# A mixture-of-experts stage with twelve weight slots instead of six, and the first two experts loaded ahead

## The chip, the core and the metric

The kernel runs on one core of one Trainium2 chip. A core has five engines that run their own instruction streams and meet at semaphores: PE (matrix products; its weight loads are listed apart as PEld), DVE (vector), ACT (activations and copies), POOL and SP, which here issues nearly all transfers from device memory. Sixteen DMA engines carry the transfers. The metric is the time of one execution in microseconds (us) on the device, a median of several.

## What is computed

One inference step of a two-layer backbone over 384 tokens (128 context, 256 latent) with a model width of 1024. Each layer is a mixer (attention and a convolution branch, merged by gates) and then a mixture of experts. All data are f32. The part that matters here is the second one:

```python
def moe(h, w_router, router_bias, w_gate, w_up, w_down):
    t = h.reshape(B * L, D)                                  # 384 x 1024
    scores = jax.nn.sigmoid((t @ w_router).astype(jnp.float32))
    ...                                                      # 1 of 4 groups, top 2 of its 4 experts
    combine = jnp.einsum('tk,tke->te', w, jax.nn.one_hot(eidx, N_EXPERTS, dtype=jnp.float32))
    hid = jax.nn.silu(jnp.einsum('td,edf->tef', t, w_gate)) * jnp.einsum('td,edf->tef', t, w_up)
    hid = hid * combine.astype(hid.dtype)[..., None]
    return jnp.einsum('tef,efd->td', hid, w_down).reshape(B, L, D)
```

There are 16 experts (0 to 15) a layer, each with a gate, an up (1024 x 512) and a down (512 x 1024) matrix: 6 MB an expert, 96 MB a layer, 192 MB in all of the 302 MB that the kernel reads.

## The kernel before

**Stages of a layer.** One hardware loop runs over the two layers, so the code of a layer stands once in every engine's program and is run twice. The stages are: adaLN (`ada`), the input projection (`qkv`, `u`, `gate`), attention with the gate products between its steps, the convolution branch, `aproj` and `cproj`, `out`, then routing (a norm, router logits, a rank of every token within its experts, and `spread`, which sorts the tokens by expert into `sortedT`), then the experts.

**Weights.** All weights pass through `ring`, six tiles of 1 MB (128 partitions x 2048 f32). The mixer's weights are cut into 48 chunks (`CHUNKS`), chunk c goes to slot c mod 6. An expert is six chunks j: gate in slots 0 and 1, up in 2 and 3, down in 4 and 5. SP issues the loads in the program's order; before each it waits until the slot's previous chunk has been used (`half` counts the uses that end in the middle of a product, `full[b]` the products that end in PSUM bank b). So chunk j of expert e waits for chunk j of expert e - 1. Expert 0 loads as the last mixer chunks are used up, in `out` and routing (L468 to L470). `landed[s]` tells PE that a slot is filled.

**An expert on PE** (`expert`, L889). Its tokens were copied by ACT to `xgT`. `products(0, 2)` multiplies them by the gate matrix, `products(1, 3)` by the up matrix, `turn_own` and `turn_hid` transpose small tiles, `down` multiplies by the down matrix. Between these, `sums` (`back`, L597) adds the rows of the expert before to the tokens' sums, so that PE doesn't wait for ACT and DVE. An expert with at most 64 tokens is *narrow* (two half-width products side by side, L557), else *wide* (L560). Since an expert's code depends on its own width and on that of the expert before, `by_width` (L370) reads two flags and branches, and the program of a pass holds four variants, in this order: narrow after narrow, narrow after wide, wide after narrow, wide after wide. Expert 0 stands in front of the loop in two variants, the loop (L919) runs experts 1 to 15, one in a pass. At its end stands the branch back.

**DVE and ACT** have loops of their own over the experts, with two variants each.

**What lies where.** `over` lays a second name on a tile that is dead by then: `hid`, `silu`, `hidT` and `own` of the expert stage lie in the convolution's tiles `csq` and `conv`, `xgT` in `probs`. The mixer's other tiles (`sig`, `hT`, `qkv`) hold nothing late in the expert stage, or only part of it.

Of the kernel before, what the change touches and what calls it, by code (L numbers as in the profile page):

```python
# [24 lines left out]
P = 128  # L25
D = 1024
# [40 lines left out]
assert NCHUNKS % SLOTS == 0  # L67
SLOT_USES = (NCHUNKS + MOE_CHUNKS * NE) // SLOTS

# [30 lines left out]

START = 3

# [28 lines left out]
def build(nc, A):  # L131
    USES, INIT, MOE_AT, PER = bank_table()
    ctx = ExitStack()
    with ctx:
        start_of = {}

        def sb(name, shape, dt=F32):
            start_of[name] = (nc.sbuf_base + 31) // 32 * 32
            return ctx.enter_context(nc.sbuf_tensor(name, shape, dt))
# [19 lines left out]
        conv = sb("conv", [P, KC, CO])  # L159
        csq = sb("csq", [P, KC, CO])  # L160
        mix = sb("mix", [P, 2 * KD * T + 4 * T])
        gates = mix[:, 0:2 * KD * T].rearrange("p (m n) -> p m n", n=T)
# [109 lines left out]

        landed = [sem(f"landed{s}") for s in range(SLOTS)]
        full = [sem(f"full{b}") for b in range(8)]
        freed = [sem(f"freed{b}") for b in range(8)]
# [141 lines left out]
        def _(sp):  # L417
# [7 lines left out]

            def load(slot, landed_sem, src):
                n = src.shape[-1]
                k = src.shape[-2]
                dst = ring[slot][:, 0:k * n].rearrange("p (k n) -> p k n", k=k)
                sp.dma_start(dst, src).then_inc(landed_sem, 16)  # L430
# [12 lines left out]
            with sp.Fori(0, DEPTH) as l:  # L443
                for c in range(NCHUNKS):
                    s = c % SLOTS
                    if c < SLOTS:

                        if c in (0, 2, 4):
                            sp.wait_ge(half, l * HALF_PER + {0: START - 2, 2: START - 1, 4: START}[c])
                        else:  # L450
                            b = {1: 2, 3: 3, 5: 6}[c]
                            sp.wait_ge(full[b], l * PER[b] + INIT[b] - (2 if c in (1, 3) else 0))
                    else:
                        wait_chunk_used(c - SLOTS, l)
                    kind, i, part = CHUNKS[c]
                    if kind == "ada":
                        src = w_ada[bass.ds(l, 1), part, :, :, i * 512:(i + 1) * 512].rearrange("o p k n -> p (o k) n")
                    elif kind in ("aproj", "cproj"):
                        w = w_ap if kind == "aproj" else w_cp
                        src = w[bass.ds(l, 1), :, :, i * 512:(i + 1) * 512].rearrange("o p k n -> p (o k) n")  # L460
                    elif kind == "router":
                        src = w_r
                    else:
                        w = w_out if kind == "out" else w_in
                        m = i + {"qkv": 0, "u": 3, "gate": 7, "out": 0}[kind]
                        src = w[bass.ds(l, 1), :, :, m * 256:(m + 1) * 256].rearrange("o p k n -> p (o k) n")
                    load(s, landed[s], src)
                for j in range(MOE_CHUNKS):  # L468
                    wait_chunk_used(NCHUNKS - SLOTS + j, l)
                    load(j, landed[j], expert_chunk(j, l * NE))  # L470

                def reload(e, first=False):
                    for j in range(MOE_CHUNKS):
                        if j in (0, 2, 4):
                            sp.wait_ge(half, l * HALF_PER + e * 3 + (12 + START - 3 + {0: 1, 2: 2, 4: 3}[j]))
                        elif j in (1, 3):
                            b = {1: 2, 3: 3}[j]
                            sp.wait_ge(full[b], lead(b, l, e - 1, first) + 1)
                        else:
                            sp.wait_ge(full[6], l * PER[6] + e + (INIT[6] + MOE_AT[6]))  # L480
                        load(j, landed[j], expert_chunk(j, l * NE + e))

                reload(1, True)
                with sp.Fori(2, NE) as e:
                    reload(e)

# [4 lines left out]
                with sp.If(over > 0):  # L491
# [3 lines left out]
                    with sp.Fori(0, BLOCKS - 1) as q:  # L495
                        with sp.Fori(0, NE) as e:
                            for j in range(MOE_CHUNKS):
# [7 lines left out]
                                load(j, landed_o[j], expert_chunk(j, l * NE + e))  # L505

# [17 lines left out]
        def _(pe):  # L524
# [20 lines left out]

            def expert_parts(n_of, lead_of, fr, fs, landed_s, land_at, half_s, own_s, own_at, xg_s, xg_at):

                def products(which, b, small):
                    pe.wait_ge(fr[b], lead_of(b))
                    pe.wait_ge(xg_s, xg_at)  # L550
                    for k in range(KD):
# [3 lines left out]
                        if small:  # L555
                            for hh in range(2):
                                last = pe.matmul(ps[64 * hh:64 * hh + 64, b, 0:256], xgT[:, k, 0:64],  # L557
                                                 ring[s][:, o + hh * 256:o + (hh + 1) * 256], start=(k == 0), stop=(k == KD - 1))
                        else:
                            last = pe.matmul(ps[:, b, :], xgT[:, k, :], ring[s][:, o:o + DE], start=(k == 0), stop=(k == KD - 1))  # L560
                        if k % 4 == 3:
# [16 lines left out]
                def down(small):  # L578
# [3 lines left out]
                    for k in range(KE):  # L582
# [3 lines left out]
                        for h in range(2):  # L586
                            w = ring[4 + s][:, c * D + h * 512:c * D + (h + 1) * 512]
                            a, z, rows = (64 * h, 64 * h + 64, hidT[:, c, 64 * s:64 * s + 64]) if small else (0, P, hidT[:, k, :])
# [34 lines left out]
            with pe.Fori(0, DEPTH) as l:  # L623
# [264 lines left out]
                settle(pe)  # L888
                def expert(e, before_e=None):  # L889
                    alone = before_e is None  # L890
                    products, turn_own, turn_hid, down = expert_parts(
                        lambda b: expert_use(b, l, e), lambda b: lead(b, l, e, alone), freed, full, landed,
                        l * (16 * SLOT_USES) + (e * 16 + 16 * 9), half, own_r, l * NE + (e + 2), xg_r, l * (NE + 1) + (e + 2))

# [30 lines left out]
                with pe.If(over > 0):  # L925
# [5 lines left out]
                    with pe.Fori(0, OSTEPS) as i:  # L931
                        products, turn_own, turn_hid, down = expert_parts(
                            lambda b: further_use(b, l, i), lambda b: further_use(b, l, i), freed_o, full_o, landed_o,
                            l * (16 * OSTEPS) + i * 16 + 16, half_o, own_r_o, l * OSTEPS + i + 2, xg_r_o, l * OSTEPS + i + 1)
# [906 lines left out]
```

## Time and profile before

| | us |
|---|---|
| three runs: median (lowest to highest) | 1324.78 (1319.63 to 1330.17) |
| the profiled execution: time | 1327.07 |
| its span (first to last instruction) | 1325.4 |
| PE busy in the span | 1187.1 |
| DVE busy | 702.0 |
| ACT busy | 433.7 |

The profile is of one execution. Stages can be told by line: L680 and L694 are the mixer's products, L878 is `spread`, L557 and L560 an expert's gate and up products, L589 its down product, L612 the sums. In the first layer the expert stage runs from 379 to 650 us, in the second from 1018 to 1293. "Chain" below is the chain of work that ended last, followed back from the end: a row is a start, a duration, and the engine and line, or the transfer, that held it. "Issue" is time in which an engine waited for nothing that the profile shows. In a timeline row the brackets hold the engine's idle time before it and what ended it. The granted clock of TensorE (PEclk) is given as a share of full speed.

### The profile page before, as it was taken

The page shows a single profiled execution, that of the slowest core. Times are in us where ns is not written, and L with a number is a line of the kernel's source. Part 1 is how long each engine was busy: PE and PEld are TensorE (multiplying, and loading weights), DVE is VectorE, ACT ScalarE, POOL GpSimd, SP SyncE. Part 2 cuts the span into 40 slices and gives each one's busy share as a digit, 9 for nine tenths or more (in the row PEclk, how much of TensorE's full clock was granted, in tenths as well). Part 3 has the DMA queues.
Part 4 walks back from the last instruction along what each step waited for, and adds up shares of the span by engine and source line. Part 5 has one row for each costly group of instructions (what it writes and reads, how often), then busy time and mean ns, then how long its engine had stood idle before and what let it go on. Part 6 is the DMA issues. An engine that isn't in the chain of part 4 may idle for free.

```text
span 1325.4 us, 20656 instructions
## 1 busy us (share of the span) xinstructions
PE 1187.1 (90%) x6340; PEld 755.7 (57%) x6341; DVE 702.0 (53%) x1425; ACT 433.7 (33%) x771; POOL 9.8 (1%) x30
## 2 busy tenths in 40 slices
PE   5999999998579999999689999999958899999973
PEld 2796555588354455444369755557926454455443
DVE  4365877664722344444566387767464234244445
ACT  2425555442331122222152345544233222122213
POOL 1000000000000000000000000000000000000000
PEclk8899999999699999999799999999978999999996
DMA  8743655423146899999783265552320889889961
GB/s 312 227 130 123 227 190 177 142 66 127 38 158 228 317 387 422 422 421 422 273 285 108 87 221 182 174 187 66 127 69 27 307 348 423 322 320 423 422 260 48
DMA packets 101983, 305.36 MB, mean 230 GB/s; under 512 B 7136, under 2 KB 47824, under 8 KB 77328
## 3 DMA queue, kind: packets, MB, share of 16 engines
q1 hardware_dynamic: 99248, 301.62, 61.0%
q10 hardware_dynamic: 2528, 2.50, 0.6%
q8 instruction: 40, 0.66, 0.2%
q14 instruction: 39, 0.32, 0.1%
q0 software_dynamic: 128, 0.26, 0.1%
HBM read 302.53 MB, written 1.84 MB: 230 GB/s over the span
## 4 chain that ended last, share of the span: by engine, by line
PE 69%; DMA 15%; DVE 8%; issue 4%; ACT 4%; DVEq 0%; SPq 0%; ACTq 0%
PE ps L694 14%; DMA ring<-in_w_e_up 13%; PE ps L557 9%; PE ps L589 6%; PE ps L560 6%; PE ps L680 5%; PE ps L715 4%; PE ps L716 3%; PE ps L717 3%; PE ps L612 3%; PE ps L878 3%; PE ps L641 2%; PE ps L653 2%; PE ps L785 2%; PE ps L760 1%
## 5 line engine op out<-in xcount | busy, mean ns | idle before, releaser
L557 PE MATMUL ps<-ring,xgT 128*64 128x256 f32 x1728 | 205.7, 387 | 16.5 <-issue 10.6
L557 PEld LDWEIGHTS ps<-ring,xgT 128*64 128x64 f32 x1728 | 125.9, 138 | 103.1 <-issue 27.7
L1420 DVE SCALAR_TENSOR_TENSOR nat<-ps,qT,nat 128x512 f32<-128x512 f32 x192 | 132.8, 745 | 80.6 <-PE ps L612 80.6
L694 PE MATMUL ps<-hT,ring 128*128 128x384 f32 x512 | 173.4, 492 | 0.0
L589 PE MATMUL ps<-ring,conv 128*64 128x512 f32 (+1 forms) x512 | 134.2, 597 | 7.2 <-issue 4.1
L1527 DVE SCALAR_TENSOR_TENSOR conv<-ub,dw,conv 128x414 f32<-128x414 f32 x240 | 136.6, 644 | 0.0
L694 PEld LDWEIGHTS ps<-hT,ring 128*128 128x128 f32 x512 | 95.4, 191 | 66.4 <-issue 7.2
L1411 DVE TENSOR_TENSOR orow_lo<-ps,orow_hi 64x512 fp32r<-64x512 f32 (+1 forms) x64 | 44.1, 689 | 112.5 <-ACT orow_hi L1037 111.7
L589 PEld LDWEIGHTS ps<-ring,conv 128*64 128x64 f32 (+1 forms) x512 | 48.3, 145 | 78.5 <-issue 78.2
L1402 DVE TENSOR_TENSOR csq<-csq,ps 128x256 f32<-128x256 f32 (+1 forms) x32 | 14.8, 463 | 129.4 <-PE ps L557 83.8
L560 PE MATMUL ps<-ring,xgT 128*128 128x512 f32 x160 | 74.8, 624 | 8.4 <-issue 8.4
L1027 ACT ACTIVATE conv<-ps 128x256 f32<-128x256 f32 (+1 forms) x32 | 13.4, 419 | 194.6 <-PE ps L575 194.6
L680 PE MATMUL ps<-ring,hT 128*128 128x256 f32 x288 | 65.9, 393 | 3.1 <-DVE hT L1377 3.1
L1037 ACT ACTIVATE orow_hi<-ps 64x512 fp32r<-64x512 f32 (+1 forms) x64 | 37.9, 593 | 87.7 <-PE ps L589 87.0
L680 PEld LDWEIGHTS ps<-ring,hT 128*128 128x128 f32 x288 | 56.8, 198 | 11.6 <-DVE hT L1377 3.4
L612 PE MATMUL ps<-orow_hi,ownT 64*128 64x512 f32 (+1 forms) x192 | 53.1, 501 | 7.6 <-DVE orow_lo L1411 4.5
L560 PEld LDWEIGHTS ps<-ring,xgT 128*128 128x128 f32 x160 | 31.2, 199 | 49.4 <-issue 48.0
L641 PE MATMUL ps<-ring,condT 128*32 128x512 f32 x384 | 51.0, 651 | 5.0 <-DMA ring<-in_w_ada 5.0
L1024 ACT ACTIVATE csq<-ps 128x256 f32<-128x256 f32 (+1 forms) x32 | 13.4, 418 | 123.8 <-PE ps L557 83.5
L715 PE MATMUL ps<-merged_hi,w_hi 128*128 128x384 f32 x128 | 43.7, 341 | 5.1 <-DVE merged_lo L1605 5.1
L878 PE MATMUL ps<-place,nat_hi 128*128 128x384 f32 x96 | 35.5, 370 | 13.7 <-DVE place L1708 13.7
L1111 ACT ACTIVATE mix<-ps 128x384 f32<-128x384 f32 x32 | 15.7, 492 | 90.2 <-PE ps L694 90.2
(254 smaller groups left out, 1797.3 us busy)
## 6 DMA issues: line engine op xcount, KB each, us to landing
ring<-in_w_e_gate SPq DMA_DIRECT2D x64, 1024.0 KB, 10.1
ring<-in_w_e_up SPq DMA_DIRECT2D x64, 1024.0 KB, 10.8
ring<-in_w_e_down SPq DMA_DIRECT2D x64, 1024.0 KB, 9.8
ring<-in_w_ada SPq DMA_DIRECT2D x48, 1024.0 KB, 7.7
ring<-in_w_in SPq DMA_DIRECT2D x30, 1024.0 KB, 6.1
ring<-in_w_out SPq DMA_DIRECT2D x8, 1024.0 KB, 5.9
ring<-in_w_attn_proj SPq DMA_DIRECT2D x4, 1024.0 KB, 5.6
ring<-in_w_conv_proj SPq DMA_DIRECT2D x4, 1024.0 KB, 6.6
```

The source lines that it names most:

```text
L557: last = pe.matmul(ps[64 * hh:64 * hh + 64, b, 0:256], xgT[:, k, 0:64], ring[s][:, o + hh * 256:o + (hh + 1) * 256], start=(k == 0), stop= ...
L560: last = pe.matmul(ps[:, b, :], xgT[:, k, :], ring[s][:, o:o + DE], start=(k == 0), stop=(k == KD - 1))
L589: last = pe.matmul(ps[a:z, 5 + h, :], rows, w, start=(k == 0), stop=(k == KE - 1))
L612: last = pe.matmul(ps[:, b, :], ownT[a:z, t * P:(t + 1) * P], rows[a:z, o:o + 512], start=first, stop=not first)
L641: last = pe.matmul(ps[32 * k:32 * k + 32, b, :], condT[:, 4 * cc + k, :], ring[c % SLOTS][:, k * 512:(k + 1) * 512], start=(cc == 0), stop ...
L680: last = pe.matmul(ps[:, b, 0:256], hT[:, k, t * P:(t + 1) * P], ring[q % SLOTS][:, k * 256:(k + 1) * 256], start=(k == 0), stop=(k == KD ...
L694: last = pe.matmul(ps[:, b, 0:T], ring[c % SLOTS][:, o:o + P], rhs(k), start=(k == 0), stop=(k == k_tiles - 1))
L715: pe.matmul(ps[:, b, 0:T], upper, hi[:, k, 0:T], start=(k == 0), stop=False)
L878: last = pe.matmul(ps[:, b, 0:HALF], part[:, t, k * P:(k + 1) * P], place[:, t, half_at * HALF:(half_at + 1) * HALF], start=(i == 0), stop ...
L1411: dve.tensor_tensor(orow_lo[a:z, o:o + 512], ps[a:z, 5 + h, :], orow_hi[a:z, o:o + 512].bitcast(F32), ALU.subtract).then_inc(fr[5 + h], 1)
L1420: dve.scalar_tensor_tensor(sums, ps[:, b, :], weight[:, t, bass.ds(at, 1)], sums, ALU.mult, ALU.add).then_inc(fr[b], 1)
L1527: dve.scalar_tensor_tensor(conv[:, i, :], src, w, conv[:, i, :], ALU.mult, ALU.add).then_inc(tapped, 1)
```

## The change

A second set of six 1 MB tiles, `odd`, is laid over tiles that are dead in the expert stage (`sig` with the start of the convolution's tiles, `probs` with what follows, `hT`, the end of `qkv`). Even experts use `ring`, odd experts `odd`, with their own semaphores `landed_odd`. Chunk j of expert e now waits for chunk j of expert e - 2. The first odd expert's chunks load as soon as what lies there is dead: after attention's last product, after `cproj`, after the second norm, after `spread`. `hid`, `silu`, `hidT`, `own` and `xgT` move to other dead places. The loops of PE and SP run over pairs of experts and hold two bodies; on PE, expert 1 stands in front of the loop as well. `START`, from which some semaphores begin to count, goes from 3 to 8, with the constants that follow from it.

```diff
-SLOT_USES = (NCHUNKS + MOE_CHUNKS * NE) // SLOTS
+SLOT_USES = NCHUNKS // SLOTS + NE // 2
...
-START = 3
+START = 8
...
-        hid = flat(csq, 0, DE)
-        silu = flat(csq, DE, 2 * DE)
-        hidT = flat(conv, 0, DE).rearrange("p (k n) -> p k n", k=KE)
-        own = flat(conv, DE, DE + NT * P).rearrange("p (t n) -> p t n", t=NT)
+        hid = over("hid", "qkv", 0, [P, DE], F32)
+        silu = over("silu", "qkv", DE, [P, DE], F32)
+        hidT = over("hidT", "qkv", 3 * D + NT * P, [P, KE, P], F32)
+        own = over("own", "hT", NT * ROWS, [P, NT, P], F32)
...
-        xgT = over("xgT", "probs", 0, [P, KD, P], F32)
+        xgT = over("xgT", "qT", 2 * NT * BLOCKS * NE, [P, KD, P], F32)
...
+        odd = [over("odd0", "sig", 0, [P, SLOT], F32), over("odd1", "sig", SLOT, [P, SLOT], F32),
+               over("odd2", "probs", 0, [P, SLOT], F32), over("odd3", "probs", SLOT, [P, SLOT], F32),
+               over("odd4", "hT", 0, [P, SLOT], F32), over("odd5", "qkv", 3 * D + NT * P + DE, [P, SLOT], F32)]
...
-                for j in range(MOE_CHUNKS):
-                    wait_chunk_used(NCHUNKS - SLOTS + j, l)
-                    load(j, landed[j], expert_chunk(j, l * NE))
-
-                def reload(e, first=False):
+                def first_even(j):
+                    wait_chunk_used(NCHUNKS - SLOTS + j, l)
+                    load(ring[j], landed[j], expert_chunk(j, l * NE))
+
+                def first_odd(j):
+                    if j == 2:
+                        b, n = use("pv", UNITS - 1, l)
+                        sp.wait_ge(full[b], n + 1)
+                    elif j < 2:
+                        b, n = use("cproj", KD - 1, l)
+                        sp.wait_ge(full[b], n + 1)
+                    elif j == 3:
+                        sp.wait_ge(xn_r, l * (2 * KD) + 2 * KD)
+                    else:
+                        b, n = use("spread", 2 * KD - 1, l)
+                        sp.wait_ge(full[b], n + 1)
+                    load(odd[j], landed_odd[j], expert_chunk(j, l * NE + 1))
+
+                first_odd(2)
+                first_even(0)
+                first_odd(0)
+                first_odd(1)
+                for j in range(1, 5):
+                    first_even(j)
+                first_odd(3)
+                first_even(5)
+                first_odd(4)
+                first_odd(5)
+
+                def reload(e, before_e, tiles, landed_s, first=False):
...
-                reload(1, True)
-                with sp.Fori(2, NE) as e:
-                    reload(e)
+                reload(2, 0, ring, landed, True)
+                reload(3, 1, odd, landed_odd)
+                with sp.Fori(2, NE // 2) as i:
+                    reload(i * 2, i * 2 - 2, ring, landed)
+                    reload(i * 2 + 1, i * 2 - 1, odd, landed_odd)
...
-                def expert(e, before_e=None):
+                def expert(e, pair, odd_one, before_e=None):
                     alone = before_e is None
+                    if odd_one:
+                        tiles, landed_s, land_at = odd, landed_odd, l * (16 * NE // 2) + (pair * 16 + 16)
+                    else:
+                        tiles, landed_s, land_at = ring, landed, l * (16 * SLOT_USES) + (pair * 16 + 16 * (NCHUNKS // SLOTS + 1))
...
-                expert(0)
-                with pe.Fori(0, NE - 1) as e:
-                    expert(e + 1, e)
+                expert(0, 0, False)
+                expert(1, 0, True, 0)
+                with pe.Fori(1, NE // 2) as i:
+                    expert(i * 2, i, False, i * 2 - 1)
+                    expert(i * 2 + 1, i, True, i * 2)
```

PE's program at the end of a loop pass, before the change: the last rows of the wide-after-wide variant (its down product), the branches out of it, and the branch back to the loop's start.

```order
L612 MATMUL ps<-orow_lo,ownT 128x512 x2
L579 REGISTER_ALU
L581 ISA x2
L589 MATMUL ps<-ring,conv 128x512 x8
L375 UNCONDITIONAL_BRANCH x2
L919 REGISTER_ALU
L919 COMPARE_AND_BRANCH
```

And of the change, the same place in the even body: behind the same down product stands not the loop's end but the odd body, with its two flag reads and branches and its first variant on the odd tiles.

```order
L628 MATMUL ps<-ring,hidT 128x512 x8
L385 UNCONDITIONAL_BRANCH x2
L382 ISA
L382 TENSOR_LOAD narrow_e
L382 ISA x2
L383 COMPARE_AND_BRANCH
L382 TENSOR_LOAD narrow_e
L382 ISA x2
L383 COMPARE_AND_BRANCH
```

The loop's end with its branch back has moved one whole body of four variants further from the loop's start, and every even expert now ends with a jump to this middle. Each of the two bodies holds four variants of the kind of which the rows below show the narrow-after-narrow one (odd tiles).

```order
L596 MATMUL ps<-odd_77,xgT 64x256 x8
L596 MATMUL ps<-odd_78,xgT 64x256 x8
L651 MATMUL ps<-orow_hi,ownT 128x512 x2
L651 MATMUL ps<-orow_lo,ownT 128x512 x2
...
L607 MATMUL ps<-ident,own 128x128 x3
...
L614 MATMUL ps<-ident,hid 128x128 x2
...
L628 MATMUL ps<-odd_81,hidT 64x512 x4
L628 MATMUL ps<-odd_82,hidT 64x512 x4
```

Its rows are those of before, with other tiles: nothing is added inside a variant, the variants are doubled.

SP's program between the router's weights and the first reload, before:

```order
L430 DMA ring<-in_w_router 128x8x16
...
L430 DMA ring<-in_w_e_gate 128x2048
...
L430 DMA ring<-in_w_e_up 128x2048
...
L430 DMA ring<-in_w_e_down 128x2048
```

and of the change (77 to 82 are the odd tiles 0 to 5):

```order
L440 DMA ring<-in_w_router 128x8x16
L486 REGISTER_ALU
L440 ISA
L440 DMA odd_79<-in_w_e_up 128x2048
L434 REGISTER_ALU
L440 ISA
L440 DMA ring<-in_w_e_gate 128x2048
L440 DMA odd_77<-in_w_e_gate 128x2048
L440 ISA
L440 DMA odd_78<-in_w_e_gate 128x2048
```

Before, six loads stood here, all of expert 0; now twelve stand here in turns, six of expert 0 and six of expert 1, and SP waits at each until its place is dead.

## Rows read from the trace of the kernel before

**Rows 1.** Page part 4: shares of the chain by engine and by line.

```profile
PE 69%; DMA 15%; DVE 8%; issue 4%; ACT 4%; DVEq 0%; SPq 0%; ACTq 0%
```

**Rows 2.** Chain in order of time, first layer's expert stage: start us, us, what.

```profile
393.39 5.97 issue
399.36 9.35 PE ps L560 x16
...
440.77 7.06 PE ps L560 x16
...
479.90 3.45 PE ps L557 x32
...
515.19 12.87 DMA ring<-in_w_e_up
...
619.55 13.00 DMA ring<-in_w_e_up
...
636.76 3.63 PE ps L589 x15
```

**Rows 3.** Chain in order of time, second layer's expert stage.

```profile
1018.04 15.71 PE ps L560 x32
...
1057.76 5.26 issue
1063.02 5.14 PE ps L557 x32
...
1088.23 3.65 PE ps L589 x16
...
1101.82 3.65 PE ps L589 x16
...
1183.32 3.45 PE ps L557 x32
...
1280.52 3.63 PE ps L589 x15
```

**Rows 4.** Busy time by stretch, columns in the first row.

```profile
core 0: us, PE busy (x) PEld busy (x) DVE busy (x) ACT busy (x) POOL busy (x), PEclk, DMA share, GB/s
20.00:370.00 350.00, 319.72 (x1582) 230.37 (x1583) 228.70 (x477) 146.01 (x264) 3.11 (x5) 0.94 0.45 151
...
399.30:426.20 26.90, 26.44 (x69) 11.38 (x69) 5.06 (x8) 3.24 (x5) 0.00 (x0) 0.92 0.58 199
...
501.00:632.60 131.60, 123.78 (x860) 63.77 (x858) 59.52 (x108) 30.57 (x54) 0.00 (x0) 1.00 1.01 422
...
281.00:377.00 96.00, 74.54 (x393) 65.56 (x391) 57.10 (x145) 31.55 (x50) 1.86 (x3) 0.88 0.21 69
```

**Rows 5.** DMA queues, whole span, then 20 to 370 us: packets, MB, share.

```profile
q8 instruction: 40, 0.66, 0.2%
...
q8 instruction: 13, 0.21, 0.2%
```

**Rows 6.** DMA queues, 393 to 399.5 us.

```profile
q8 instruction: 2, 0.03, 2.7%
```

**Rows 7.** DMA queues, 399.5 to 440 us.

```profile
q8 instruction: 2, 0.03, 0.3%
```

**Rows 8.** DMA queues, 440 to 650 us, all rows.

```profile
q1 hardware_dynamic: 13456, 83.47, 98.3%
q14 instruction: 3, 0.02, 0.0%
```

**Rows 9.** DMA queues, 1057 to 1063 us.

```profile
q8 instruction: 1, 0.02, 0.9%
```

**Rows 10.** Timeline of SP's queue, 280 to 400 us: two loads of each kind.

```profile
289.54 11.47 SPq L430 DMA_DIRECT2D ring<-in_w_e_gate  x2
...
382.39 2.68 SPq L430 DMA_DIRECT2D ring<-in_w_e_gate  x2
```

**Rows 11.** Timeline of PE, where the layer loop turns back.

```profile
657.88 0.71 PE L628 MATMUL ps<-ident,prow 76*128 76x76 f32 x2 [3.18 <-DVE xT L1791]
```

More of the change, by code:

```diff
@@ L160, in build @@
         csq = sb("csq", [P, KC, CO])
+        gap = sb("gap", [P, 16])
         mix = sb("mix", [P, 2 * KD * T + 4 * T])
@@ L273, in build @@
         landed = [sem(f"landed{s}") for s in range(SLOTS)]
+        landed_odd = [sem(f"landed_odd{s}") for s in range(SLOTS)]
         full = [sem(f"full{b}") for b in range(8)]
@@ L424, in wait_chunk_used, with load @@
                     sp.wait_ge(full[b], n + 1)
-            def load(slot, landed_sem, src):
+            def load(tile, landed_sem, src):
                 n = src.shape[-1]
                 k = src.shape[-2]
-                dst = ring[slot][:, 0:k * n].rearrange("p (k n) -> p k n", k=k)
+                dst = tile[:, 0:k * n].rearrange("p (k n) -> p k n", k=k)
                 sp.dma_start(dst, src).then_inc(landed_sem, 16)
@@ L466, in _ @@
                         src = w[bass.ds(l, 1), :, :, m * 256:(m + 1) * 256].rearrange("o p k n -> p (o k) n")
-                    load(s, landed[s], src)
-                for j in range(MOE_CHUNKS):
+                    load(ring[s], landed[s], src)
+                def first_even(j):
                     wait_chunk_used(NCHUNKS - SLOTS + j, l)
-                    load(j, landed[j], expert_chunk(j, l * NE))
-                def reload(e, first=False):
+                    load(ring[j], landed[j], expert_chunk(j, l * NE))
@@ L476, in reload @@
                         elif j in (1, 3):
                             b = {1: 2, 3: 3}[j]
-                            sp.wait_ge(full[b], lead(b, l, e - 1, first) + 1)
+                            sp.wait_ge(full[b], lead(b, l, before_e, first) + 1)
                         else:
-                            sp.wait_ge(full[6], l * PER[6] + e + (INIT[6] + MOE_AT[6]))
-                        load(j, landed[j], expert_chunk(j, l * NE + e))
-                reload(1, True)
-                with sp.Fori(2, NE) as e:
-                    reload(e)
+                            sp.wait_ge(full[6], l * PER[6] + before_e + (INIT[6] + MOE_AT[6] + 1))
@@ L488, in _ @@
+                        load(tiles[j], landed_s[j], expert_chunk(j, l * NE + e))
+                reload(2, 0, ring, landed, True)
[3 more added lines that the diff above has]
+                    reload(i * 2 + 1, i * 2 - 1, odd, landed_odd)
                 sp.wait_ge(pos_r, l + 1)
@@ L504, in _ @@
                                     sp.wait_ge(full_o[b], l * (OSTEPS * back_to) + q * (NE * back_to) + e * back_to + 1)
-                                load(j, landed_o[j], expert_chunk(j, l * NE + e))
+                                load(ring[j], landed_o[j], expert_chunk(j, l * NE + e))
                     sp.wait_ge(full_o[6], l * OSTEPS + (OSTEPS + 1))
@@ L557, in products @@
                                 last = pe.matmul(ps[64 * hh:64 * hh + 64, b, 0:256], xgT[:, k, 0:64],
-                                                 ring[s][:, o + hh * 256:o + (hh + 1) * 256], start=(k == 0), stop=(k == KD - 1))
+                                                 tiles[s][:, o + hh * 256:o + (hh + 1) * 256], start=(k == 0), stop=(k == KD - 1))
                         else:
-                            last = pe.matmul(ps[:, b, :], xgT[:, k, :], ring[s][:, o:o + DE], start=(k == 0), stop=(k == KD - 1))
+                            last = pe.matmul(ps[:, b, :], xgT[:, k, :], tiles[s][:, o:o + DE], start=(k == 0), stop=(k == KD - 1))
                         if k % 4 == 3:
@@ L586, in down @@
                         for h in range(2):
-                            w = ring[4 + s][:, c * D + h * 512:c * D + (h + 1) * 512]
+                            w = tiles[4 + s][:, c * D + h * 512:c * D + (h + 1) * 512]
                             a, z, rows = (64 * h, 64 * h + 64, hidT[:, c, 64 * s:64 * s + 64]) if small else (0, P, hidT[:, k, :])
```

17 lines of the change are left out of this document (10 added, 7 removed).

## The prediction

> **What bounds the kernel now.** I read the chain of waits first: PE holds 69% of the span and transfers 15%, and nearly all of the transfers are one line, `ring<-in_w_e_up`, a weight load of the expert loop [rows 1]. So only the expert stage waits for weights, and I read that stage in order of time.
>
> In the first layer experts 1 and 3 are wide (L560), the rest narrow. From 515.19 to 619.55 the chain shows eight waits for an up-projection chunk, one per expert, seven steps of (619.55 - 515.19) / 7 = 14.9 us [rows 2]. In that stretch the DMA engines are full: 422 GB/s, share 1.01 [rows 4]. So 14.9 us is what six 1 MB chunks take, and the stage is transfer-bound there. Before it, it is not: from one narrow expert's down-projection to the next, 1088.23 to 1101.82, are 13.59 us with only PE rows in the chain [rows 3]. That is the whole room: **a narrow expert costs 14.9 us behind transfers and 13.59 us behind PE.**
>
> Two holes in the same stage are neither: 5.97 us at 393.39 between experts 0 and 1 of the first layer, 5.26 us at 1057.76 between experts 1 and 2 of the second, both marked "issue" [rows 2, 3]. They are not late weights: expert 1's gate chunks were issued from 382.39 [rows 10], and 11 us at this rate are over four chunks. What does fall into both holes is a packet or two on q8, the queue that brings instructions [rows 6, 9]. I take them for PE waiting for its program; the rest of the forecast hangs on that.
>
> **How PE gets its program, as the trace shows it.** 20 to 370 us has no loop: 1582 matmuls and 1583 weight loads ran and 13 packets of 16 KB came [rows 4, 5]. That is 243 records a packet, about 256 with waits and register instructions; I call that a block. A plain f32 matmul row of the program leaves two matmuls and two weight loads in the trace, the others one of each. So a narrow variant of an expert (40 plain rows, 17 others) is 194 records, about 217 instructions, a wide one (24 and 19) about 157. A pass of the loop of before has four variants: about 767 instructions, 3.0 blocks.
>
> First passes: in the first layer PE leaves expert 0's narrow code and leaps over some 570 instructions to "wide after narrow": hole of 5.97 and two packets [rows 2, 6]. In the second it leaves "narrow after wide" and leaps over both wide variants, some 320 instructions, to the loop's end: hole of 5.26 and one packet [rows 3, 9]. A leap over one variant left no hole: expert 1's wide code to the loop's end, 157. So what is fetched ahead is about one block; a leap past it waits. After the first passes nothing is fetched again: two packets more up to 440 [rows 7], none from 440 to 650 [rows 8], ten and more passes. A pass of three blocks stays in PE's store.
>
> **The change, part by part.**
>
> *Twelve slots: takes the transfer-bound stretches away.* Chunk j of expert e+2 can now load as soon as expert e has used its slot, so transfers may run a whole expert ahead. Fourteen experts after the start are 14 x 14.9 = 209 us, the stage is over 260; behind wide experts, which take some 25 us, the transfers gain 10 us on PE and then lose 1.3 us per narrow one, at most 12 x 1.3 = 16 us, less than the expert they may be ahead. So PE sets the pace throughout. First layer: 479.90 to 636.76 + 3.63 = 640.39 is 160.5 us for experts 5 to 15; at 13.59 it is 149.5: **-11.0**. Second layer: 1183.32 to 1280.52 + 3.63 = 1284.15 is 100.8 for seven; at 13.59 it is 95.1: **-5.7** [rows 2, 3]. Together -16.7.
>
> *First two experts loaded early: 0.* The six extra loads fall into 281 to 377 us, where the queue moves 69 of 422 GB/s [rows 4]; expert 0's were there already, from 289.54 [rows 10], and expert 1 waits for no weights now, as shown above. SP's new waits (attention's last product, cproj's last, the norm, the last spread) hold back only loads that wait for something later anyway: behind the last of them stand expert 2's, which need expert 0's products. If that cover were gone, a chunk is 14.9 / 6 = 2.5 us.
>
> *Tiles laid elsewhere, next layer's first w_ada loads one expert earlier: 0.* DVE's and ACT's programs keep their instructions and waits.
>
> *Two bodies in PE's loop, and expert 1 written out in front of it: new first-pass holes.* A pass is now about 1530 instructions, 6.0 blocks, and has a middle as well as an end to leap to. First layer:
> - expert 0 to 1: some 565 instructions, as before: 0.
> - 1 to 2: over one variant: 0.
> - 2 to 3: "narrow after wide" (even) leaps over both wide variants to the middle, some 320, as at 1057.76: 5.3. Then, in the odd body, over both narrow variants (434) to "wide after narrow": the block after the first, and the one after that. One hole of 5.97 if they come together, two of 5.3 if one after the other; I take 8.
> [...]
>
> Second layer (experts 0 wide, 1 to 5 narrow): 1 to 2 leaps over both wide ones, as before: 0 more. Expert 2 is "narrow after narrow", the first variant of the even body, and leaps over the other three (531) to the middle: 5.97; expert 3 the same in the odd body to the loop's end: 5.97. Clock: a narrow first product takes 5.14 instead of 3.45 [rows 3], 1.7 twice. Sum 15.3. First layer 5.3 + 8 + 2.3 = 15.6. Together **+30.9**.
>
> Sum: 1325.4 - 16.7 + 30.9 = **1339.6, say 1340 us**. The median of the three runs, 1324.78, is within a microsecond of this span.
>
> *Bounds of the holes.* Below: nothing, since two of the fetches up to 440 cost nothing, PE's queue running ahead of them; then 1308.7. The nearest cheaper row is the 3.18 us of PE at 657.88, where the layer loop turns back [rows 11]: five blocks at that price plus 5.7 for the clock are 21.6, 1330. Above: every leapt block by itself at 5.3, and expert 1's entry one block worse: three blocks, 2.3 and 5.3 in the first layer, four blocks and 3.4 in the second: 48, 1357. The value taken is that of the rows with like leaps under like traffic.
>
> **Rivals.**
> - *No new holes* (faster). PE's queue runs ahead far enough, or the holes were something that the change doesn't multiply: 1325.4 - 16.7 = 1308.7. For it: the leap of 157 behind a wide expert. Against it: narrow experts, from which the new leaps start, left two of two in the open. It decides for "faster" if the new holes sum to less than 3.5 us.
> - *Cheap holes*: 1330, by the row at 657.88. For it: there the queues were not full of weights. Against: in the expert stage they are.
> - *The pass doesn't stay in PE's store* (much slower). A pass of 6.0 blocks touches seven, and one more is fetched ahead; the trace shows five held, no more. If the first are gone at the loop's turn, each pass has two holes of 5.97, one of 5.3 and three slow products: 22.3 us, twelve more passes in two layers: 268, some 1600. Against it: nothing was fetched twice so far.
>
> [...]
>
> **How the numbers follow.** Likeliest 0.55 (1332 to 1357 by itself), no new holes 0.16, cheap ones 0.14, refetching 0.15. The range 1309 to 1357 leaves out refetching and a tail of the first rival. One per cent, about what can be told here from no change, is 1312 to 1338. Faster: most of the no-hole case, 0.11. Same: the rest of it, the cheap case and two fifths of the likeliest, 0.41. Slower: three fifths of the likeliest and refetching, 0.48. The likeliest case ends just above the bound.
>
> **What would show it.** In the profile after: no `in_w_e_up` waits in the chain; narrow experts 13.6 us apart to the end of both layers; "issue" holes of 5 to 6 us between experts 2 and 3 in both layers and behind 3 in the second, with q8 packets in them; some 52 q8 packets in all (40 now plus six blocks a layer), against some 130 if passes are refetched. The forecast is wrong if the holes are missing, if transfers still wait in the chain, or if q8 keeps running past expert 4.

## The result and the profile after

| | before | changed |
|---|---|---|
| median (lowest to highest) of four runs each on one chip, us | 1325.71 (1319.63 to 1330.17) | 1341.45 (1334.31 to 1345.60) |
| the profiled execution: time, us | 1327.07 | 1334.31 |
| its span, us | 1325.4 | 1332.7 |

The ratio is 1.0129, 95% interval 1.0100 to 1.0158: the changed kernel is slower by about 1.3%, where 1340 us was forecast. The profiled execution of the changed kernel is the quickest of its four, so its rows account for 7.3 us of a difference of 15.7 us in the medians. A second profile, among the experiments, shows where more of it lies.

First the page of the changed kernel: its share of the chain by engine, which answers to [rows 1], and its instruction queue, which answers to [rows 5] (packets, MB, share).

```profile
PE 82%; DVE 7%; issue 5%; ACT 3%; DMA 2%; DVEq 0%; SPq 0%; ACTq 0%
...
q8 instruction: 52, 0.85, 0.3%
```

The transfers fell from 15% of the chain to 2%, and no up-projection load is left in it. "Issue" rose by a point, and twelve more packets of program came. Next the chain of the changed kernel in order of time (start us, us, what), first layer's expert stage, which answers to [rows 2]. Its L596, L599 and L628 are L557, L560 and L589 of before.

```profile
380.23 8.81 PE ps L596 x64
...
394.43 5.33 issue
399.76 9.36 PE ps L599 x16
...
440.87 11.47 issue
452.34 8.67 PE ps L599 x16
...
611.69 3.65 PE ps L628 x16
...
625.28 3.65 PE ps L628 x16
...
638.86 3.63 PE ps L628 x15
```

The old hole between experts 0 and 1 is there (5.33), and a new one between experts 2 and 3, 11.47 us long. Later the narrow experts follow each other at 625.28 - 611.69 = 13.59 us, the pace of PE, in place of the 14.9 us behind transfers. The second layer, which answers to [rows 3]:

```profile
1018.38 15.71 PE ps L599 x32
...
1058.09 3.40 issue
1061.49 3.67 PE ps L596 x32
...
1075.30 5.75 issue
1081.05 6.56 PE ps L596 x32
...
1097.74 5.59 issue
1103.33 5.67 PE ps L596 x32
...
1287.78 3.63 PE ps L628 x15
```

Two new holes, behind experts 2 and 3, and behind each a first product of 5.7 to 6.6 us where 3.45 is normal. The instruction queue of the changed kernel from 440.9 to 452.3 us, the hole of the first layer:

```profile
q8 instruction: 4, 0.07, 2.7%
```

From 473.25 to 649.5 us, nearly all the rest of the first layer's stage, the same view has no q8 row, only these:

```profile
q1 hardware_dynamic: 11985, 71.10, 99.0%
q14 instruction: 2, 0.02, 0.0%
```

So the code is fetched once a layer and then stays: in the second layer no q8 row stands from 1110 to 1290 us either. The busy time of the stretch that [rows 4] show of before (us, PE busy, PEld, DVE, ACT, POOL, granted clock, DMA share, GB/s):

```profile
501.00:632.60 131.60, 129.70 (x936) 73.92 (x935) 64.65 (x118) 33.67 (x60) 0.00 (x0) 1.00 1.01 422
```

PE is busy 129.7 of 131.6 us, where it was 123.8. The transfers run as full as before, but now they run ahead of PE and nothing waits for them.

**Where the time went.** I measure the expert stage from the start of expert 0's first product (the L596 x64 and L599 x32 rows) to the end of the last down product (the x15 rows), in the chain of each profile:

| profile | first layer, us | second layer, us | sum | span |
|---|---|---|---|---|
| before | 261.2 | 266.1 | 527.3 | 1325.4 |
| changed | 262.3 | 273.0 | 535.3 | 1332.7 |
| changed, second profile | 262.3 | 276.3 | 538.6 | 1336.5 |
| changed, late loads | 262.1 | 279.8 | 542.0 | 1342.9 |
| before, two bodies | 273.2 | 278.8 | 552.0 | 1349.7 |
| before, short branches | 253.4 | 259.2 | 512.6 | 1311.6 |
| changed, short branches | 242.7 | 253.7 | 496.4 | 1291.5 |

The span less both stages is 798.1 us before and 797.4 after: whatever the change moved outside the expert stages costs nothing that can be seen.

### The profile page after: what moved, and what is told of

The parts are those of the page before. It is cut to its first block, busy times and chain, and to the rows that moved or that the text cites. A ratio compares the mean times of both kernels' runs of the same rounds, so it can differ in the third digit from the quotient of the medians.

```text
span 1332.7 us, 20562 instructions
## 1 busy us (share of the span) xinstructions
PE 1184.2 (89%) x6340; PEld 761.8 (57%) x6341; DVE 702.3 (53%) x1425; ACT 434.0 (33%) x771; POOL 9.7 (1%) x30
## 4 chain that ended last, share of the span: by engine, by line
PE 82%; DVE 7%; issue 5%; ACT 3%; DMA 2%; DVEq 0%; SPq 0%; ACTq 0%
PE ps L596 15%; PE ps L733 14%; PE ps L628 10%; PE ps L599 6%; PE ps L651 5%; PE ps L719 5%; PE ps L754 4%; PE ps L755 3%; PE ps L756 3%; PE ps L917 3%; PE ps L680 3%; PE ps L692 2%; PE ps L824 2%; PE ps L799 1%; PE ps L869 1%
## 5 line engine op out<-in xcount | busy, mean ns | idle before, releaser
L596 PE MATMUL ps<-ring,xgT 128*64 128x256 f32 x896 | 106.2, 391 | 11.0 <-issue 11.0
L596 PE MATMUL ps<-odd,xgT 128*64 128x256 f32 x832 | 98.1, 389 | 5.8 <-issue 5.8
L596 PEld LDWEIGHTS ps<-ring,xgT 128*64 128x64 f32 x896 | 68.2, 141 | 51.3 <-issue 26.5
L596 PEld LDWEIGHTS ps<-odd,xgT 128*64 128x64 f32 x832 | 64.0, 140 | 42.0 <-issue 20.3
L1447 DVE TENSOR_TENSOR hid<-silu,ps 128x256 f32<-128x256 f32 (+1 forms) x32 | 14.8, 463 | 119.6 <-PE ps L596 73.9
L1072 ACT ACTIVATE hidT<-ps 128x256 f32<-128x256 f32 (+1 forms) x32 | 13.4, 418 | 185.2 <-PE ps L614 185.2
L628 PE MATMUL ps<-odd,hidT 128*64 128x512 f32 (+1 forms) x256 | 68.8, 597 | 2.9 <-issue 2.2
L628 PE MATMUL ps<-ring,hidT 128*64 128x512 f32 (+1 forms) x256 | 65.4, 597 | 4.0 <-ACT hidT L1072 2.1
L599 PE MATMUL ps<-odd,xgT 128*128 128x512 f32 x96 | 46.4, 639 | 16.8 <-issue 16.8
L628 PEld LDWEIGHTS ps<-odd,hidT 128*64 128x64 f32 (+1 forms) x256 | 25.1, 146 | 39.6 <-issue 38.7
```

The source lines that it names most:

```text
L599: last = pe.matmul(ps[:, b, :], xgT[:, k, :], tiles[s][:, o:o + DE], start=(k == 0), stop=(k == KD - 1))
L628: last = pe.matmul(ps[a:z, 5 + h, :], rows, w, start=(k == 0), stop=(k == KE - 1))
```

## Experiments

**Theory.** The change is two changes. The twelve slots are worth some 17 us; the way PE's program was written for them, two long bodies a pass, costs some 25 to 31 us in first passes, because branches leap over code that has not been fetched yet. **Rival:** the holes belong to the weights (odd tiles, earlier loads, late chunks). The expectations count the experts from the first, which is expert 0.

### The code without the slots: two bodies in the kernel before

```diff
-                with pe.Fori(0, NE - 1) as e:
-                    expert(e + 1, e)
+                expert(1, 0)
+                with pe.Fori(1, NE // 2) as i:
+                    expert(i * 2, i * 2 - 1)
+                    expert(i * 2 + 1, i * 2)
```

> The kernel before with six slots and its old loads; only the code of TensorE's expert loop is changed: two experts' bodies in one pass of the loop, and the second expert in front of it. No weight comes earlier or later by design. Theory (holes are code that is not yet on the chip): the long branch leaps of a first pass come back in a new place, as in the changed kernel: in the first layer one hole of 8 to 13 us before the fourth expert, in the second layer two of 5 to 6 us, each with 1.5 to 3 us of low clock behind it; since the rest of the stage is bound by the transfers, part of it is soaked up: 1335 to 1352 us, ratio 1.008 to 1.02, some 50 instruction packets on TensorE's queue. Rival (the holes belong to the new buffers and late weights): no new hole, 1325 us, ratio 0.998 to 1.002.

Measured: 1350.89 us against 1323.87 for the kernel before on the same chip, ratio 1.0205 (1.0167 to 1.0244), 52 instruction packets. Its chain, first and second layer:

```profile
438.57 11.50 issue
450.08 8.76 PE ps L560 x16
...
525.81 12.71 DMA ring<-in_w_e_up
...
1088.80 4.48 issue
...
1109.65 5.44 issue
```

With six slots and the old loads the holes appear between the same experts and at nearly the same lengths as in the changed kernel (11.50 for 11.47; 4.48 and 5.44 for 5.75 and 5.59). So the holes come with PE's code, not with the new tiles. The stages grew by 12.0 and 12.7 us, where the new holes, the slow products behind them and what changed in the old ones sum to 12.9 and 13.5. So the transfers that bind the rest of the stage (12.71 at 525.81) soaked up less than a microsecond in each, and the part of the expectation on soaking up was wrong. A transfer waits for a slot that PE frees late, which may be why; no run singles that out.

### The same work in short branches

Each step of an expert gets a two-way branch of its own, in place of one choice among four whole variants: seven two-way branches an expert in place of two. A pass shrinks by half (in the changed kernel from some 1530 to some 790 instructions), and no branch leaps far. Made twice, on the changed kernel and on the kernel before:

```diff
-                    if alone:
-                        by_width(pe, e, lambda small: whole(small, None))
-                    else:
-                        by_width(pe, e, lambda small: by_width(pe, before_e, lambda small_before: whole(small, small_before)))
+                    narrow = pe.value_load(narrow_e[0:1, bass.ds(e, 1)], min_val=0, max_val=1)
+                    if not alone:
+                        narrow_before = pe.value_load(narrow_e[0:1, bass.ds(before_e, 1)], min_val=0, max_val=1)
+                    def either(flag, step):
+                        with pe.If(flag > 0):
+                            step(True)
+                        with pe.Else():
+                            step(False)
+                        pe.nop()
...
+                    either(narrow, lambda small: products(0, 2, small))
+                    add_before(0)
+                    either(narrow, lambda small: products(1, 3, small))
+                    add_before(1)
+                    turn_own()
+                    either(narrow, turn_hid)
+                    add_before(2)
+                    either(narrow, down)
```

> The changed kernel; only TensorE's code is changed: instead of four whole variants of each expert (wide or narrow after wide or narrow), each step of an expert has its own two-way branch, so that a pass has some 790 instructions instead of 1530 and no branch jumps over more than some 70. Theory (long jumps over code not yet fetched): all idle time of kind issue between the experts 1 to 4 goes, in both layers, with its low clock (11.5 + 1.6 + 5.3 in the first, 5.8 + 5.6 + 3.4 + 5.3 in the second, 38 us of the quickest run): 1296 to 1306 us. If the added branches themselves cost 0.1 to 0.3 us each and lie bare (about 7 more per expert, 32 experts): 1320 to 1365. Rival (the holes are late weights or rows): they stay, about 1341.

> The kernel before with the same short branches on TensorE and nothing else. Theory: the old holes of the first experts go (6.0 in the first layer, 5.3 in the second, with 3 to 4 us of low clock), and the steady experts stay at the pace of the transfers, which also hides the added branches: 1308 to 1318 us, ratio 0.987 to 0.994. Rival (those holes are something else): 1325, ratio 0.998 to 1.002.

Measured on the same chip: 1294.23 us for the changed kernel with short branches, 2 us below the expected range, ratio to before 0.9779 (0.9744 to 0.9813); 1313.23 for the kernel before with them, ratio 0.9907 (0.9870 to 0.9944). The chain of the changed kernel with short branches, where the holes were:

```profile
389.15 3.65 PE ps L628 x16
392.81 7.07 PE ps L599 x16
...
428.53 3.58 PE ps L628 x16
432.11 7.06 PE ps L599 x16
...
481.38 3.65 PE ps L628 x16
...
495.00 3.65 PE ps L628 x16
```

Expert 1's first product follows expert 0's last at once and takes 7.07, not 9.36; expert 3 follows expert 2 at once. The steady step, 495.00 - 481.38 = 13.62 us for 13.59, shows that the five branches more an expert cost next to nothing. In the kernel before with short branches the same places are closed, and the transfers are the bound from 511 us on, their waits ending at 523.91 and 538.83, at the old step of 14.9 us:

```profile
511.42 12.49 DMA ring<-in_w_e_up
...
525.94 12.89 DMA ring<-in_w_e_up
```

These four kernels split the result. Slots: 1294.23 - 1313.23 = -19.0 us in the medians, -10.7 and -5.6 in the stages. Code: +24.7 us in the stages of the two-body kernel. Their sum, -16.3 + 24.7 = +8.4, is what the changed kernel's profile shows, +8.0. And the version with both, slots and short branches, beats the kernel before by 2.2%.

### Early loads of the second expert taken back

```diff
-                first_odd(2)
-                first_even(0)
-                first_odd(0)
...
+                for j in range(6):
...
+                b, n = use("spread", 2 * KD - 1, l)
+                sp.wait_ge(full[b], n + 1)
+                for j in range(6):
+                    first_odd(j)
```

> The changed kernel with the second expert's six loads all issued after the spread, behind the first expert's six, instead of between them. Theory (loading the second expert early is worth nothing, since it waits for the code and then lags behind by one expert): as the changed kernel within 3 us, 1338 to 1345 us. Rival (the early load carries part of the time): the second expert waits for its weights about 10 us in each layer, 1350 to 1361 us, with idle time that ends by a DMA in the chain before the second expert.

Measured: 1343.43 us, ratio 1.0133 (1.0087 to 1.0179), where the changed kernel has 1.0129. SP's timeline of this kernel shows all six loads between 378.30 and 381.6:

```profile
378.30 0.86 SPq L440 DMA_DIRECT2D odd<-in_w_e_gate  x2
...
380.48 1.09 SPq L440 DMA_DIRECT2D odd<-in_w_e_down  x2
```

The first layer's stage is 262.1 us against 262.3. A wait of expert 1 for its weights could still be hidden by the hole in front of it, so the same edit was made where that hole is gone, on top of the short branches:

> Both edits together: short branches on TensorE, and the second expert's six loads issued only after the spread, behind the first expert's. Without the hole in front of it the second expert starts 7 us earlier than in the changed kernel, so its weights could now be the last thing to come. If early loading is worth nothing even then (six loads issued at 378 land two or three us apart, the gate chunks before the first expert is done at 393): as with early loads, 1292 to 1299 us, no transfer in the chain between the first two experts. If it carries something: a wait that a transfer ends in front of the second expert, 3 to 12 us a layer, 1300 to 1318 us. If it is worth less than nothing (the early loads take transfer time from the mixer's last weights): 1280 to 1291 us.

Measured: 1295.67 us, ratio 0.9789 (0.9753 to 0.9825), against 1294.23 and 0.9779 with early loads, and no transfer in the chain between the first two experts. Loading the second expert early is worth nothing here in either form: the other six slots are free after the spread, and six loads issued then are in time.

### The variants in another order

The even body's variants in reverse order of code, wide after wide first:

```diff
...
+                            with pe.If(narrow < 1):
+                                step(False)
+                            with pe.Else():
+                                step(True)
...
-                    expert(i * 2, i, False, i * 2 - 1)
+                    expert(i * 2, i, False, i * 2 - 1, turned=True)
```

> The changed kernel with the four variants of the even experts' body in the opposite order of code (wide after wide first, narrow after narrow last); the work is the same. Theory (a hole stands where a branch leaps over code that is not there yet): in the second layer the third expert's variant now ends where the fourth expert's code begins, so the hole of 5.75 us between them goes, and one of 8 to 12 us opens between the second and the third, where there were 3.4 us, since three variants are leapt over there; the one behind the fourth expert stays (5 to 6, or 12 us). In the first layer a hole of 4 to 8 us opens between the second and third expert, where there was none, and that between the third and fourth shrinks from 11.5 to 4 to 8 us. Time 1333 to 1350 us. Rival (the place in the order of experts decides, by weights or rows): holes stay between the same experts at the same lengths.

Measured, one execution: 1336.18 us (the changed kernel on that chip 1338.11). The chain of this kernel:

```profile
443.22 5.60 issue
...
1053.01 11.01 issue
...
1076.39 3.65 PE ps L628 x16
1080.05 3.45 PE ps L596 x32
...
1093.63 10.97 issue
```

The holes moved with the code, at the same experts, weights and rows. In the second layer expert 3 (1080.05) follows expert 2 at once, where 5.75 us stood; in front of expert 2 the hole grew from 3.40 to 11.01. In the first layer the one behind expert 2 shrank from 11.47 to 5.60. One part missed: in front of the first layer's expert 2 a hole of 4 to 8 us was expected, and none came, though three wide variants are leapt there (expert 1's own last one and two of the body). Expert 1 is wide in that layer and takes some 26 us. A packet of program moved at 423.91, 4.8 us before it was done, so the fetch may have been hidden behind its work; no run tests that.

### A pass longer by a fifth, never run

```diff
...
+                            for _ in range(75):
+                                pe.matmul(ps[:, 2, :], xgT[:, 0, :], tiles[0][:, 0:DE], start=True, stop=True)
...
```

It stands in the even body's wide-after-wide variant, which this data never takes.

> The changed kernel with 75 more matmuls (300 instructions) in one variant of the loop's even body that this data never takes, so that nothing more is computed: a pass grows from 1530 to 1831 instructions of code. If the store of TensorE's code still holds the whole pass: as the changed kernel, 1335 to 1352 us, 53 to 58 instruction packets on TensorE's queue, none late in a loop. If the pass no longer fits: packets in every pass, 100 to 170 in all, holes in the chain in each of the seven passes, 1450 to 1600 us. [...]

Measured, one execution: 1557.41 us, 219 us above the changed kernel on that chip, and 149 packets instead of 52. Its chain in the first layer, long after the first pass, and its instruction queue from 520 to 671 us:

```profile
520.15 6.48 issue
526.62 5.53 PE ps L596 x32
...
542.28 12.71 issue
...
593.15 12.52 issue
...
643.99 11.84 issue
```

```profile
q8 instruction: 27, 0.44, 1.5%
```

From the middle of the first layer's third pass on (520.15), and in the passes of the second layer, the code is fetched again, and PE waits at the middle and at the end of a pass. One pass of narrow experts, from 593.15 to 643.99, is 50.84 us, where two steps of 13.59 are 27.18: with the slow products a refetched pass costs 23.7 us more. (The 219 us are 18 a pass over the twelve passes behind the first ones of the two layers.) One part missed: holes were expected in each of the seven passes, but the first layer's second pass (experts 4 and 5) ran without a hole, and no packet moved from 473 to 520 us. Why that pass was spared stays open. Otherwise a pass of some 1530 instructions stays (no packet from 473.25 to 649.5 us in the changed kernel), and one of some 1830 doesn't (27 packets from 520 to 671 us here). The longer leap in the even body is not all of it: behind the odd body (12.52 at 593.15), whose own leaps are as long as before, PE waits as well, though the jump back from there is longer too.

### The holes without weight traffic

The loads of the experts 2 to 15 cut to 64 of 2048 columns:

```diff
-                        load(tiles[j], landed_s[j], expert_chunk(j, l * NE + e))
+                        sp.dma_start(tiles[j][:, 0:64], expert_chunk(j, l * NE + e).rearrange("p o n -> p (o n)")[:, 0:64]
+                                     ).then_inc(landed_s[j], 16)
```

> The changed kernel with the loads of the experts 2 to 15 (in each layer, first loop over the experts) cut to 64 of 2048 columns per slot, so that the products there use old weights and the output is not the reference's; no weight traffic is left in that stretch from the third expert's loads on. Theory (the holes are code fetches, the traffic of the weights only makes them longer): holes between the same experts, shorter: 6 to 8 us in place of 11.5 before the fourth expert of the first layer, 3 to 4.5 in place of 5.6 to 5.8 in the second; 52 instruction packets; 1320 to 1332 us. Second reading of the same theory (the fetch takes its time whatever the traffic): lengths as before, 1333 to 1345. Rival (the holes are late weights): none left, 1300 to 1310.

Measured, one execution: 1310.17 us, 52 packets. Its chain in both layers:

```profile
393.68 2.64 issue
...
436.91 5.99 issue
...
1061.89 2.49 issue
1064.38 3.67 PE ps L597 x32
...
1078.18 2.99 issue
```

The same code is fetched, and the holes stay behind the same experts at about half the length: 2.64 for 5.33, 5.99 for 11.47, 2.49 and 2.99 for 5.75 and 5.59, and of the 3.40 only 0.63 is left. So a hole is not a wait for weights, but beside weights it is longer. The DMA share in the four holes that are over 2 us is 0.07 to 0.10 here; in the changed kernel it was 0.54 in the long hole of the first layer (last rows of this document) and 0.97 to 1.01 in the three of the second. The packets show where the time goes. In the second layer expert 3's first product follows a packet by 5.0 us here (packet at 1059.35) and by 4.6 us in the changed kernel (packet at 1076.48). But here the packet moves 2.5 us before expert 2 is done, and there 1.2 us after. So the weights seem to hold a fetch up before its packet moves; what holds it no row names.

The time came out 10 us below the expected range and at the edge of the rival's (1300 to 1310); what rules the rival out are the holes that are left. Holes and slow products together shrank more than I had thought, 24.2 us in the two stages against the second profile, a third of it at one place (10.92 there, 2.99 here). One slow product grew: 9.85 us behind the hole of 5.99, 8.67 behind that of 11.47.

### The changed kernel once more

> The changed kernel once more, for a second profile, since the profiled execution was the quickest of its four (1334.3 us, the others 1341.3 to 1345.6). If the difference lies in the fetches: one of the holes of the first passes is longer by a second fetch (11 to 12 us in place of 5.6, as behind the fourth expert of the second layer in the kernel whose second expert is loaded late), with the same 52 packets, and a time of 1339 to 1346 us. If it lies elsewhere: holes as in the first profile (11.5; 3.4, 5.8, 5.6) at a time above 1339.

Measured: 1338.11 us with 52 packets. The chain of this second profile:

```profile
441.24 11.24 issue
...
1075.91 4.68 issue
...
1096.05 10.92 issue
```

The holes are within 1.1 us of the first profile's but for one: behind the second layer's expert 3 stand 10.92 us instead of 5.59. The time is a microsecond below the expected range. The kernel with late loads shows 11.93 there, at 1344.49 us. So the same program waits there once for one fetch and once, it seems, for two. The packets fit: in the first profile one of the three around this place moved at 1092.29, 5.5 us before expert 3 was done, in the second at 1095.84, 0.2 us before. That explains 5.3 us of what the first profile lacks against the median; the rest of the 7 us, and why the fetch starts earlier in one execution than in another, stays open.

## Why the prediction was right

**The bound and the gain (-16.7): right.** The chain has no up-projection load left, and the experts step at 13.59 us to the end of both layers. In the changed kernel experts 5 to 15 of the first layer take 149.4 us and experts 9 to 15 of the second 95.1, which is -11.1 and -5.8 (forecast -11.0 and -5.7). Measured apart from the code, by the two kernels with short branches, the slots are worth -10.7 and -5.6 us in the stages.

**Early loads (0) and moved tiles (0): right,** by the two kernels with late loads, by the 798.1 and 797.4 us outside the stages and by the step of 13.59 us, which is that of before.

**The first-pass holes (+30.9): right in kind and place, a little large in both profiles.** Behind expert 2 of the first layer the forecast took 5.3 to get to the middle and 8 to get to the variant, 13.3 us; with this order of code and the weights it was 11.23 to 11.50 in every profile, two fetches of some 5.7. The slow product behind it cost 1.6 us (8.67 for 7.06), where the sum has 2.3, which is 9.35 less 7.06 of [rows 2], at a granted clock of 0.92 from 399.3 to 426.2 us [rows 4]. In the second layer 5.97 twice was forecast: 5.75 or 4.68 behind expert 2, and 5.59 or some 11 behind expert 3, which makes the difference between executions; the products cost 3.1 and 2.2 for 1.7 each. What I took for unchanged got shorter: the hole in front of the second layer's expert 2 went from 5.26 to 3.40, and its product from 5.14 to 3.67. In the first profile all this sums to 12.4 + 13.3 = 25.7 us, in the second to some 29. One zero rests on a wrong count: from expert 1 to 2 of the first layer PE leaps over two variants, expert 1's last one and the body's first (some 374 instructions by the forecast's sizes), and not over one. No hole came there, nor in the turned kernel, where it leaps over more. The twelve packets more came as forecast, six blocks a layer. That is about all of the code that was added (two bodies of some 767 instructions), though PE ran only one of expert 1's four variants in each layer; so code that is leapt over seems to be fetched too. The choice that I called the one on which all hangs, that an "issue" hole with packets in it is missing code, was the right one.

**No new holes (1308.7): fell,** and with it "something that the change doesn't multiply": the holes came with the two bodies alone. The changed kernel with short branches lies below these 1308.7, at 1294, because there the old holes go too: 5.97 and 5.26 us with 2.3 and 1.7 of slow products are 15.2 us.

**Cheap holes (1330): fell for the reason given.** The cheaper price at 657.88, 3.18 us, was put down to queues without weights. With the weights taken away the holes in the expert stage cost 2.5 to 3.0 us each (one only 0.63), and 5.99 where two fetches follow each other.

**Refetching (some 1600): did not happen, but by a margin of a fifth of the pass at most.** Its price was well sized: 22.3 us for each of twelve later passes was forecast, and a refetched pass of the padded kernel lost 23.7 us. That all twelve would be refetched was not borne out there: the first layer's second pass was spared. No row of before shows how long a pass may get before it is fetched again, so the chance of 0.15 was my estimate.

**The sum** landed at 1340 for 1341.45. Its terms were each within some 5 us, and their errors partly cancel: the second fetch behind the second layer's expert 3 was not forecast as such, nor were the old holes' shorter times. So the place and kind of the loss are the prediction's merit, and the last few microseconds are luck.

## What to carry to other kernels

Count the instructions that a change adds to an engine's loop as you count bytes and columns: here two bodies with whole variants for each case, some 1530 instructions a pass, cost 24.7 us in first passes (two bodies, six slots) and left the later steps of the changed kernel at 13.59 us, and at some 1830 a pass of two experts cost 23.7 us more nearly every time. Where a branch only chooses between forms of a step, branch at the step: here that cost nothing measurable and was worth some 11 us before and some 47 us after the change, in the medians (14.7 and 38.9 us in the stages of the first profiles). And when a change that should help loses, split it: half of this one was worth 19 us and the other half cost more.

## What was new about the hardware

- A pass of some 1530 instructions ran seven times on one fetch. One of some 1830 was fetched again in nearly every pass, at 23.7 us a pass and 219 us more in all.
- A leap over missing code cost 2.5 to 3.0 us with a DMA share of 0.08 to 0.10 (one, with 0.04, only 0.63) and 3.4 to 7 us beside weight loads; what look like two in a row cost 6 and 11 to 13 (one hole of the padded kernel was 16.36).
- The same leap in the same program cost 5.59 us in one execution and 10.92 in the next.
- A stall of 3.40 us left the next narrow product at 3.67 us, one of 3.69 (two bodies, six slots) left it at 5.36, one of 5.75 at 6.56 (3.45 without a stall). Over the hole of 3.40 the granted clock stayed at 1.00; over that of 5.75 it was 0.92, and 0.55 over the product behind it. It fell while PE stood still and was not back when the work was: by stretch, the changed kernel's hole of 11.47 us and the 13.7 us behind it, with the granted clock third from the end (it was 1.00 up to 445 us, 0.50 from 447 to 454 and 1.00 again from 456):

```profile
440.87:452.34 11.47, 0.00 (x1) 0.00 (x1) 2.06 (x5) 1.19 (x2) 0.00 (x0) 0.69 0.54 204
452.34:466.00 13.66, 13.66 (x30) 5.90 (x31) 1.41 (x2) 0.60 (x1) 0.00 (x0) 0.89 0.46 154
```
